# Two products instead of three in three late stages, paired modulation sums, and the work around them in another order

## The reference, cut to what matters

```
# first block (only its first kind of layer is reached here)
u  = rmsnorm(x) * norm_pre
y  = rglru_mixer(u)          # u @ a_w_in, short convolution, gates, scan, @ a_w_out
h  = x + rmsnorm(y) * norm_post
x  = h + sigmoid(h @ ple_w_gate) * (p @ ple_w_proj)
# second block
mod = silu(c) @ w_mod + b_mod          # 12288 numbers: six vectors of 2048
h   = rmsnorm(x)*(1 + sc_m) + sh_m     # sh_m, sc_m, ga_m, sh_f, sc_f, ga_f = split(mod)
i, ff, fb, q, g, cv, cg, gc, gh = split(h @ w_in)
y_h = (rmsnorm(scan(q, i, ff, fb)) * silu(g)) @ hgrn_out_w      # "hout", 1024 -> 2048
y_c = conv_branch(cv, cg) @ conv_pw_w                            # "pw"
y   = (sigmoid(gc)*y_c + sigmoid(gh)*y_h) @ w_out                # "wout", 2048 -> 2048
x   = x + ga_m * rmsnorm(y)
x   = x + ga_f * rmsnorm(relu(h2 @ mlp_w1)**2 @ mlp_w2)          # h2 = modulated rmsnorm(x)
```

## Time and profile before

| what | value |
|---|---|
| median of three executions | 2158.94 us |
| the profiled execution: its own time | 2158.34 us |
| the profiled execution: span from first to last instruction | 2156.6 us |
| TensorE busy / VectorE (DVE) busy / ScalarE (ACT) busy / GpSimd (POOL) busy | 98% / 74% / 47% / 4% |
| moved by DMA | 448 MB, mean 208 GB/s |

### The profile page before, as it was taken

The page is one execution under the profiler, slowest core; times in us unless marked ns, Lnnn a source line. Parts: engine busy times, 40 slices in busy tenths (PEclk is TensorE's granted clock), DMA queues, the critical chain, the costliest instruction groups (busy, mean ns, idle before and its releaser), DMA issues.

```text
span 2156.6 us, 34209 instructions
## 1 busy us (share of the span) xinstructions
PE 2112.1 (98%) x14048; PEld 1899.8 (88%) x14048; DVE 1589.5 (74%) x2377; ACT 1006.8 (47%) x1495; POOL 84.9 (4%) x75
## 2 busy tenths in 40 slices
PE   7999999999999999999999999999999999999997
PEld 7787899798988888999999999968888888888886
DVE  6778699688889876577787789786766766656655
ACT  6766344546522322444554444454444434434443
POOL 1000002020000000000000000100000000000012
PEclk9999999999999999999999999999999999999998
DMA  6656778686733466444446988846775675555552
GB/s 223 204 200 226 250 251 273 221 275 220 249 117 121 161 207 233 138 137 138 137 128 221 344 290 297 322 136 195 256 254 189 227 244 192 182 194 193 189 179 95
DMA packets 122411, 447.96 MB, mean 208 GB/s; under 512 B 13712, under 2 KB 13840, under 8 KB 121872
## 3 DMA queue, kind: packets, MB, share of 16 engines
q1 hardware_dynamic: 122256, 445.78, 61.7%
HBM read 441.53 MB, written 4.19 MB: 207 GB/s over the span
## 4 chain that ended last, share of the span: by engine, by line
PE 69%; DVE 3%; ACT 1%; issue 1%; POOL 0%; POOLq 0%; ACTq 0%; DVEq 0%
PE bank L809 68%; DVE AR L1534 1%; DVE AR L1454 1%; DVE WL L1447 1%; DVE AR L1447 1%; DVE SR L1454 0%; PE bank L933 0%; PE bank L964 0%; ACT AR L1072 0%; ACT L1072 0%; ACT WH L1071 0%; POOL AR L2000 0%; ACT AR L1071 0%; DVE SR L1447 0%; POOL AR L2002 0%
## 5 line engine op out<-in xcount | busy, mean ns | idle before, releaser
L809 PE MATMUL bank<-SR,WH 128*128 128x256 f32 (+1 forms) x8128 | 1863.4, 324 | 25.5 <-DVE WL L1447 16.8
L809 PEld LDWEIGHTS bank<-SR,WH 128*128 128x128 f32 x8128 | 1289.3, 191 | 85.4 <-issue 27.8
L809 PE MATMUL bank<-SR,WL 128*128 128x256 f32 (+1 forms) x5088 | 1309.8, 290 | 0.2 <-DVE SR L1454 0.2
L809 PEld LDWEIGHTS bank<-SR,WL 128*128 128x128 f32 x5088 | 968.8, 190 | 104.7 <-DVE SR L1454 0.7
L1447 DVE TENSOR_TENSOR WL<-WF,WH 128x1024 fp32r<-128x1024 f32 x636 | 773.0, 1227 | 214.3 <-ACT WH L1071 213.8
L1071 ACT ACTIVATE WH<-WF 128x1024 fp32r<-128x1024 f32 x636 | 671.0, 1057 | 481.6 <-PE bank L809 435.6
L1454 DVE SCALAR_TENSOR_TENSOR AR<-WF,SM,AR 128x512 f32<-128x512 f32 x345 | 256.2, 763 | 8.0
L1447 DVE TENSOR_TENSOR AR<-AR 128x256 f32<-128x256 f32 (+9 forms) x382 | 163.0, 457 | 58.4 <-ACT AR L1072 36.4
L1071 ACT ACTIVATE AR<-bank 128x256 f32<-128x256 f32 (+2 forms) x199 | 80.0, 414 | 239.3 <-PE bank L809 226.1
L1995 POOL TENSOR_TENSOR AR<-AR 128x256 f32<-128x256 f32 x56 | 67.9, 1213 | 2040.0 <-ACT AR L1072 2039.9
L1447 DVE TENSOR_TENSOR AR<-AR,bank 128x256 f32<-128x256 f32 x112 | 47.2, 421 | 115.3 <-PE bank L809 89.1
(11 more groups left out here) (72 smaller groups left out, 455.8 us busy)
## 6 DMA issues: line engine op xcount, KB each, us to landing
WF<-in_mlp SPq DMA_DIRECT2D x256, 512.0 KB, 4.4
WF<-in_mod SPq DMA_DIRECT2D x192, 512.0 KB, 4.9
WF<-in_w_in SPq DMA_DIRECT2D x176, 512.0 KB, 4.4
WF<-in_a_in SPq DMA_DIRECT2D x64, 512.0 KB, 4.7
WF<-in_a_out SPq DMA_DIRECT2D x32, 512.0 KB, 4.9
WF<-in_ple_g SPq DMA_DIRECT2D x32, 512.0 KB, 4.8
WF<-in_w_out SPq DMA_DIRECT2D x32, 512.0 KB, 5.6
WF<-in_pw SPq DMA_DIRECT2D x16, 512.0 KB, 3.6
```

Of the source, the lines that this page charges most:

```text
L809: return tensor.matmul(o, l, r, start=start, stop=stop, skip_group_check=True)
```

## The change

1. `HALVES` also names hout, gh and wout, all but the last tile of wout (`WHOLE`). Their evacuation becomes: ACT copies the second half, DVE adds the first half and frees the bank (`after` step 1), and the old work (sigmoid, square, scaling) comes in later steps; gh has four such steps where it had two.
2. Modulation groups 8 to 19, 22 and 23 are summed in pairs: the weights are laid out anew so that a block holds one row of 1024 columns for two groups, and DVE does one instruction of 1024 columns per block in place of two of 512. The pause in `add_mod` comes once per pair, and a pair is closed at once.
3. At the start, x pieces and weight blocks are loaded in another order and the parameters after them; the low part of the first block is issued before the third and fourth tile of x; the first block's products run first all with WH and then all with WL; the ticks in the second half of the first quad are gone.
4. `readout` takes eight parts instead of seven: its reciprocal of 512 columns is two of 256 in two parts, and the last subtraction comes one part later.
5. `add_y2` works in eight groups of two tiles, five on DVE through PSUM and three on POOL, in the order of `LAST`, in which the last two entries have changed places.

```diff
-HALVES = ("mlp1", "mlp2")
-AFTER = {..., "gc": 1, "gh": 2, "mlp1": 2}
+HALVES = ("hout", "gh", "wout", "mlp1", "mlp2")
+WHOLE = ("wout", 15)
+AFTER = {..., "gc": 1, "hout": 1, "gh": 4, "wout": 2, "mlp1": 2}
+PAIRED = tuple(range(8, 20)) + (22, 23)
-LAST = [(0, "v"), (2, "v"), (10, "p"), (4, "v"), (12, "p"), (6, "v"), (14, "p"), (8, "v")]
+LAST = [(0, "v"), (2, "v"), (10, "p"), (4, "v"), (12, "p"), (6, "v"), (8, "v"), (14, "p")]
...
-            if mods and mods[0] % 8 == 0 and not paused[0] and mods[0] > 64:
+            if mods and mods[0] in lone and not paused[0] and mods[0] > 64:
...
         if kind == "xb":
             make(2)
             prepare(ahead=0)
+            low_parts()
...
-                else:
-                    tick(8)
...
+            for part in ("high", "low") if kind == "xb" and b == 0 else ("both",):
...
-    for q in range(len(XPIECES)):
-        steps.append(("load_x", q))
-        steps.append(("load", q))
-        st["issued"] += 1
-        if q == 2:
-            steps.append(("load_params",))
+    for what in ("x", "w", "x", "w", "x", "w", "w", "x", "w", "x"):
...
+    steps.append(("load_params",))
...
 # product
-            if kind in HALVES:
+            if kind in HALVES and what != WHOLE:
 # ACT, evac
+                if kind == "wout" and what != WHOLE:
+                    act(YO1[:, j, :], cross(what), ACT.Copy).then_inc(half_a, 1)
+                    return
-                act(YH[:, j, :], ps, ACT.Copy).then_inc(leave, 1)
+                act(YH[:, j, :], cross(what), ACT.Copy).then_inc(half_a, 1)
-                act(SQ[j % 2], ps, ACT.Sigmoid).then_inc(leave, 1)
+                act(SQ[j % 2], cross(what), ACT.Copy).then_inc(half_a, 1)
 # ACT, after
+            elif kind == "gh" and n == 2:
+                act(SQ[j % 2], SQ[j % 2], ACT.Sigmoid).then_inc(gh_a, 1)
+            elif kind == "wout" and n == 2 and (kind, j) != WHOLE:
+                square(SQUARES[kind], j, YO1[:, j, :])
+                act(YO1[:, j, :], YO1[:, j, :], ACT.Copy, scale=gga[:, j:j + 1])
 # DVE, after
+            elif kind in ("hout", "gh", "wout") and n == 1 and (kind, j) != WHOLE:
+                w.wait_ge(half_a, COPIED[kind] + j + 1)
+                tt(s, psum((kind, j)), s, ALU.add).then_inc(left((kind, j))[0], 1)
 # DVE, mod_sum
+            if cg in PAIRED:
+                    o = stt(MA2, f, c, MA2, ALU.mult, ALU.add)
 # DVE, readout
-            inverse(f"ro{pr}")
-            yield
+            mark(vector.reciprocal(rs[:, 0:T], rs[:, 0:T]))
+            yield
+            vector.reciprocal(rs[:, T:2 * T], rs[:, T:2 * T]).then_inc(st_rs, 1)
 # DVE, add_y2 (POOL does the same for the "p" entries, with two instructions on SBUF)
-                mark(tt(YO1[:, k:k + 4, :], YO1[:, k:k + 4, :], rs_b(RSTD[0], 4), ALU.mult))
-                tt(XT2[:, k:k + 4, :], XT2[:, k:k + 4, :], YO1[:, k:k + 4, :], ALU.add).then_inc(x3_v, 1)
+                    tt(z, YO1[:, at:at + 2, :], rs_b(bank[5][:, 0:T], 2), ALU.mult).then_inc(z_x3, 1)
+                    tt(XT2[:, at:at + 2, :], z, XT2[:, at:at + 2, :], ALU.add).then_inc(x3_v, 1)
```

## The result

The kernel after takes **2150.42 us** (median of 5 executions, 2148.95 to 2151.91) against 2158.75 us for the kernel before, timed beside it. The ratio is 0.9962, 95% interval 0.9951 to 0.9973: faster by 8.3 us (0.4%), where 9.2 were forecast. The profiled execution took 2150.5 us, with a span of 2148.5 us (before 2158.34 and 2156.6).

A forecast was written before the change was run, and what follows sets the result against it. TensorE was taken as the bound, busy 2112.1 of 2156.6 us. Terms -7.4 + 0.6 + 1.3 - 2.2 - 0.5 - 0.4 - 0.6 = -9.2 gave a median of 2149.7 us, range 2144.5 to 2155.5.

The forecast's parts named there:

- A step of two costs 0.348 us: hout, gh, wout: 624 steps each fall from 0.360 to 0.348 us with two matmuls, -7.4 us in all.
- The rule of the Trainium skill: Rival for hout, gh, wout: the per-column rule holds, the conversion gives 1.6 instead of 7.4 us, 2155.5 us; chance 0.04.
- The wide sum: DVE's modulation sum of 1024 columns: 1.29 us by extended slope, bounds 1.22 and 1.50; hout's DVE load 43.3 us.
- Short waits in hout and early wout, +0.6: hout and early wout: TensorE waits briefly because DVE is 97% loaded, +0.6 us, bounds 0 and 5.3.
- From gh to wout, +1.3: Start of wout: a longer chain makes the third weight block's low part late, +1.3 us, bounds 0.5 and 3.
- the wait moves to the bank: Rival, mainly hout and early wout: late bank release costs up to 0.79 us per tile, 2169.5 us at 25 tiles; chance 0.06.
- readout, -2.2: readout: split reciprocal and later subtractions let the scan's instruction come 1.1 us earlier each time, -2.2 us, bounds 0 and -3.5.
- The start, -0.5: First blocks: earlier first matmul nearly cancelled by small-parameter work moving behind the quad, -0.5 us, bounds -3.1 and +1.5.
- From wout to mlp1, -0.4: Between wout and mlp1: a 0.8 us wait goes, four transposes add 0.44, -0.4 us, bounds -0.8 and +1.
- The end, -0.6: Last stores: POOL's part comes last and its store starts one issue earlier, -0.6 us, bounds -0.3 and -0.7.
- full side terms: Rival at start and readout: early start fully kept and both readout waits gone, 2145.8 us; chance 0.16.
- DVE did not starve a stage: Rival for the new stages: wide sum at upper bound, hout at DVE's pace, gh-to-wout stall 3 us, 2153.8 us; chance 0.19.

The follow-up runs named there:

- e1: Kernel after with hout, gh and wout back to three matmuls per step and their old evacuation; 2153.45 us.
- e9: Kernel after with three edits: after-steps issued before prepare, ticks back in the first quad, fourth modulation block after the reciprocal of x3; 2143.8 us.
- e10: e9 with hout, gh and wout back to three matmuls a step; 2149.51 us.
- e5: Kernel after with the due after-steps in hout, gh and wout issued ahead of block splitting and modulation sums; 2146.23 us in one execution.
- e12: e9 with the last two readout subtractions on DVE one part later, in a ninth part; 2141.74 us.
- e7: Kernel after with the ticks back in the second half of the first quad; 2147.75 us in one execution.
- e8: Kernel after with the fourth modulation block between wout and mlp1 placed after the reciprocal of x3; 2147.12 us in one execution.
- e4: Kernel after with the old seven-part readout and the old order of the last stores; 2152.62 us in one execution.
- e3: Kernel after without paired modulation groups, so sums of 512 columns and a pause and close per group; 2151.47 us.
- e2: Kernel before with only the conversion of hout, gh and wout to two matmuls per step and the split evacuation; 2155.74 us.
- e6: e5 with the modulation blocks of wout beginning one call later; 2147.95 us in one execution.
- e11: e9 without pairs, all modulation sums 512 columns wide; 2145.74 us in one execution.

## Why the prediction held, and where its steps did not

The total was forecast at -9.2 and came to -8.3 us. Some of the steps were off in both directions.

- **A step of two costs 0.348 us: right.** hout is 44.60 us for 128 steps, and e1 has 0.360 in the same place. The rule of the Trainium skill (TensorE: Matmul & The Clock Gate, Back-to-back issue gap) gives an estimate of 1.6 us for all of it; e9 and e10 show 6.8. The measured step decides.
- **The wide sum: the value right, its working not.** Forecast 1.29 us. But 0.33 us more for 256 more columns, carried on for 512 more, gives 0.75 + 0.66 = 1.41 us and not 1.29. By that value hout's load on DVE would have come out near 45 us, over TensorE's 44.6, so the nearness of 1.29 to the measured 1.285 is luck. By shapes, the group on DVE of the kernel after:
```profile
L1491 DVE SCALAR_TENSOR_TENSOR AR<-WF,SM,AR 128x1024 f32<-128x1024 f32 x105 | 135.0, 1285 | 4.2
```
- **Short waits in hout and early wout, +0.6: wrong, there are none.** DVE was busy for 41.78 and not 43.3 us in hout, and TensorE never waited. The working adds whole lengths, while neighbouring instructions on DVE overlap: in the rows above, the addition at 1304.19 starts 0.09 us before the two at 1303.40, 0.88 us long together, end.
- **From gh to wout, +1.3: the stall came, with another cause and size.** I let the low part of wout's third block end it. It was the bank: 0.90 us of idle at 1229.36 and 1.79 at 1304.71, 3.2 us of gh's time by e5 (2.8 net of the delays that e5 then shows in wout). This is the rival "the wait moves to the bank", true at two places and not at the 12 that it needed to turn the sign; it had a chance of 0.06. I reasoned about how many tiles pass until a bank comes round, and not about what stands in DVE's queue in front of one addition at the worst moment: two wide sums or a pair's close. The first place, inside gh, I had not seen at all.
- **Why the three stages together still came out as forecast** (-5.44 against -5.5, which is -7.4 + 0.6 + 1.3): the bank took 3.2 instead of 1.9 us, and wout gave 1.3 us more than its 240 steps. Of that, 0.88 is eight transposes that are no longer in the window (777 instructions before, 768 of them the steps' matmuls; now 528, the steps' alone), and 0.25 is idle time that it had the earlier trace rows. Two errors of opposite sign cancelled, and that is luck.
- **readout, -2.2: half, -1.1.** The step that failed is "the last subtractions and the wait for ACT come after the scan's operations". They left the place ahead of the first of these and still stood ahead of the second, behind which TensorE waits (e9); moved behind that too, they give another 1.3 us (e12).
- **The start, -0.5: measured -0.24.** The first matmul came at 7.58 us, near the 7.2 said. The stall at 20.78 was to shrink; it came at 14.45 with 2.28 instead of 2.59 us. 3.64 us at 50.92 took nearly all of the rest back. The cause given, small parameters on DVE, carries 1.4 us (e7).
- **From wout to mlp1, -0.4: measured -0.22**, bound by TensorE's own work there as said: taking 1.9 us of it out of the way brought 2.0 (e8). **The end, -0.6: measured -0.63** (e4). In the kernel after, POOL's last operation and SP's stores:
```profile
2144.75 1.26 POOL L2075 TENSOR_TENSOR AR<-AR 128x512 f32<-128x512 f32 x1
...
2140.03 6.34 SPq L819 DMA_DIRECT2D out<-AR  x8
```
- **Not foreseen: cv, ff and fb, -0.67.** I took the wide sums there for free, since TensorE hides them. They take a low-part wait of 0.75 down to 0.24 us in cv; with PAIRED = () it is back (e3).

The other rivals: full side terms did not come, and DVE did not starve a stage (by its own terms that rival's sum is 2153.5 and not 2153.8 us). What stays open is the second half of the start, the wait at 40.46 us in e7.

## What to carry to other kernels

When a change puts an operation between a finished tile and the release of its PSUM bank, issue that operation ahead of everything that isn't urgent on the engine, and look for the longest thing that can stand in front of it; here the order alone decided whether the conversion was worth 4.0 us (e1) or 6.8 us (e10) over the three stretches. A wait is cut only by moving work past the last instruction that the waiter needs, not past the first. Work that fills TensorE during a dependency chain belongs after the last matmul of that chain: here it cost 2.0 us in front of it and nothing behind it.

## What the runs showed of the hardware that I had not expected

TensorE's granted clock fell to half (1.2 GHz) behind short idle times, and not the same in each run. After the 1.78 us wait at 1106 it was 0.50 for 3.41 us in e4, and likewise in e2, but 1.00 in the kernel before after 1.79 us. Behind the idle time before mlp1, the kernel after:
```profile
1413.78:1420.61 6.83, 5.95 (x19) 5.11 (x20) 5.63 (x11) 3.70 (x7) 0.00 (x0) 0.50 0.18 61
```
In e9 the same place, after 2.22 us of idle time, for half as long:
```profile
1409.47:1412.88 3.41, 3.41 (x12) 2.98 (x13) 2.39 (x5) 2.42 (x4) 0.00 (x0) 0.55 0.10 38
```
At the start (14 to 20 us) it was 0.72 in the kernel after, e7 and e10, and 0.50 in e9. mlp1's first half took 92.96 us in the kernel after and 92.1 to 92.2 in e1, e5, e7, e8 and e9, with the same work. The length of the idle time before does not tell these apart: after 4.02 or 4.03 us the halved stretch was 6.8 us long in the kernels before and after, e2 and e6, and 3.4 in e1, e3, e4, e5 and e7; after 2.21 or 2.22 us it was 3.4 us long in e8, e9 and e10 and absent in e11 and e12. Nor does each cost time: in e12 TensorE waits 1.25 us for DVE at 1414.00 instead, and mlp1's first half, from very first matmuls, takes 92.13 us against 92.28 in e9, and 93.29 in the kernel after. Where it does cost, such a stretch is worth 1 to 2 us, as much as most of the edits here. The spans alone could not have told them apart; the table by stretch could.
